# Token inputs laid out by features, the first modulation in two column groups, and a third gate block ahead of the context

## The reference

```python
mx = (silu(c) @ ada_w + ada_b).reshape(6, D)        # modulation of the tokens
mc = (silu(c_ctx) @ ada_w + ada_b).reshape(6, D)    # and of the context
hx = rmsnorm(x,   norm1_g) * (1 + mx[1]) + mx[0]    # x   [512, 1024]
hc = rmsnorm(ctx, norm1_g) * (1 + mc[1]) + mc[0]    # ctx [256, 1024]
ux, uc = hx @ w_in, hc @ w_in                       # gates, values, queries, ...
oc, sc_f, sc_b = hgrn_bidir(*hgrn_inputs(uc, lb), s_zero, s_zero)
ox, _, _       = hgrn_bidir(*hgrn_inputs(ux, lb), sc_f, sc_b)
x = x + mx[2] * merge_branches(ux, hgrn_readout(ux, ox, ...), ...)
x = x + mx[5] * conv_ffn(modulate(rmsnorm(x, norm2_g), mx[3], mx[4]), ...)
x = rmsnorm(x, final_g)
```

## Time and profile before

| | |
|---|---|
| median of three timed runs | 2410.75 us (2410.43 to 2411.60) |
| profiled execution | 2411.24 us |
| its span | 2409.5 us |
| PE busy | 2305.6 us, 96% |
| PEld (weight loads) busy | 1862.6 us, 77% |
| DVE busy | 1395.6 us, 58% |
| ACT busy | 874.8 us, 36% |
| POOL busy | 162.6 us, 7% |
| HBM read | 270.57 MB, 113 GB/s over the span |
| mean granted TensorE clock | 0.984 |

### The profile page before, as it was taken

One profiled execution on the slowest core, in us unless ns is written; L12 is line 12 of the kernel. 1 busy time (PEld: TensorE's weight loads), 2 busy tenths in 40 slices (PEclk: granted clock), 3 DMA queues, 4 the chain that ended last, 5 costly groups with the idle time before them and its releaser, 6 DMA issues.

```text
span 2409.5 us, 29333 instructions
## 1 busy us (share of the span) xinstructions
PE 2305.6 (96%) x10276; PEld 1862.6 (77%) x10276; DVE 1395.6 (58%) x2056; ACT 874.8 (36%) x1168; POOL 162.6 (7%) x96
## 2 busy tenths in 40 slices
PE   7999999989999989999999998999998998999998
PEld 3788888768887868787778776888886886888886
DVE  4556856669999766654745547555435445333322
ACT  4533433245554333323323234443223233443322
POOL 0000000026664000000000000000000000000000
PEclk9999999999999999999999998999999999999999
DMA  6442214413334624142332323666532332333322
GB/s 270 131 136 74 71 57 151 152 57 105 89 102 140 192 80 146 55 129 88 104 116 74 106 79 124 192 190 199 157 93 65 105 96 63 105 94 104 96 88 70
DMA packets 72944, 273.82 MB, mean 114 GB/s; under 512 B 8096, under 2 KB 8480, under 8 KB 71456
## 3 DMA queue, kind: packets, MB, share of 16 engines
q1 hardware_dynamic: 53424, 199.74, 26.7%
q10 hardware_dynamic: 19440, 72.96, 9.6%
HBM read 270.57 MB, written 2.10 MB: 113 GB/s over the span
## 4 chain that ended last, share of the span: by engine, by line
PE 90%; DVE 5%; issue 2%; ACT 2%; DMA 1%; ACTq 0%; DVEq 0%; POOL 0%; SPq 0%
PE bank L424 85%; PE bank L765 1%; PE bank L862 1%; DVE rstd L472 1%; DVE rv_lo L1979 0%; DVE hx_lo L480 0%; PE bank L455 0%; DMA ident<-in_ident 0%; DVE tnorm L487 0%; PE bank L659 0%; PE bank L457 0%; DVE rstd L1799 0%; DVE std L449 0%; DVE rt L1930 0%; PE bank L944 0%
## 5 line engine op out<-in xcount | busy, mean ns | idle before, releaser
L424 PE MATMUL bank<-hx_hi,w_hi 128*128 128x512 f32 x1792 | 711.6, 397 | 40.2 <-DVE hx_lo L480 35.0
L424 PE MATMUL bank<-hx_hi,w_lo 128*128 128x512 f32 x1792 | 704.0, 393 | 0.0
L424 PE MATMUL bank<-hx_lo,w_hi 128*128 128x512 f32 x1792 | 703.9, 393 | 0.0
L383 DVE TENSOR_TENSOR w_lo<-w_raw,w_hi 128x1024 fp32r<-128x1024 f32 x306 | 374.8, 1225 | 495.2 <-ACT w_hi L375 488.9
L375 ACT ACTIVATE w_hi<-w_raw 128x1024 fp32r<-128x1024 f32 x350 | 369.0, 1055 | 458.1 <-PE bank L424 416.3
L424 PEld LDWEIGHTS bank<-hx_hi,w_hi 128*128 128x128 f32 x1792 | 340.7, 190 | 116.6 <-issue 41.1
L424 PEld LDWEIGHTS bank<-hx_hi,w_lo 128*128 128x128 f32 x1792 | 339.9, 190 | 72.4
L424 PEld LDWEIGHTS bank<-hx_lo,w_hi 128*128 128x128 f32 x1792 | 340.6, 190 | 71.0 <-issue 1.2
L1859 DVE SCALAR_TENSOR_TENSOR bank<-zpad,cols,bank 128x512 f32<-128x512 f32 x352 | 233.8, 751 | 11.7 <-ACT bank L1388 11.7
L424 PE MATMUL bank<-hid_hi,w_hi 128*128 128x512 f32 x528 | 210.1, 398 | 1.5 <-POOL hid_lo L2156 1.5
L424 PE MATMUL bank<-hid_lo,w_hi 128*128 128x512 f32 x528 | 209.8, 397 | 0.0
(11 more groups left out here) (305 smaller groups left out, 2752.3 us busy)
## 6 DMA issues: line engine op xcount, KB each, us to landing
w_raw<-in_wstream SPq DMA_DIRECT2D x350, 512.0 KB, 3.6
ada_raw<-in_ada_nk ACTq DMA_DIRECT2D x128, 512.0 KB, 3.7
ada_w<-in_ada_kn SPq DMA_DIRECT2D x8, 1024.0 KB, 18.8
dec<-in_dec ACTq DMA_DIRECT2D x4, 960.0 KB, 4.6
x_tok<-in_x SPq DMA_DIRECT2D x1, 2048.0 KB, 7.8
out_x<-out_tok SPq DMA_DIRECT2D x4, 512.0 KB, 4.0
crow<-in_crow SPq DMA_DIRECT2D x3, 512.0 KB, 23.1
ctx_tok<-in_ctx SPq DMA_DIRECT2D x1, 1024.0 KB, 9.9
```

The source lines that it names most:

```text
L383: nc.vector.tensor_tensor(w_lo[nb.at % RING][:], w_raw[nb.at % RAW][:], w_hi[nb.at % RING][:].bitcast(F32), ALU.subtract).then_inc(lo_read ...
L424: ins = nc.tensor.matmul(out_ap, s, m, start=first and at == 0, stop=last and at == n - 1)
```

## The change

- x, ctx and ctx_2 are stored on the host with features first, in the layout of res, ctx_t and ctx2_t, and loaded there. All transposes of tokens and the copies behind them go (`turn_pe`, jobs 0 to 3 of `context_pe`), and so do the counts "turn" and "turn2".
- The first modulation weights are stored as two column groups (half 0: features 0 to 511 of shift and scale; half 1: the rest) and come in 11 pieces. PE does half 0 for all k, then half 1; before k = 3 of half 1 it sums the squares of x and turns the rows of half 0 (`ada0_turn(0)`). The rows of half 1 are turned inside the first pair, before its k = 2.
- DVE makes modulation and x tiles 0 to 3 for half 0, then 4 to 7 for half 1. ACT has the x tiles in two groups and the context squares between the tiles of the second.
- POOL makes w_lo of the first two blocks and the sums of the context squares. ACT splits weight blocks 0, 1 and 2 at places between the other steps.
- Gate block 2 for x goes into bank bw[0] (third_gate) between the first pair and the context of blocks 0, 1, 2. The context's norm is summed after the pair.
- Of crow, row C is loaded first and gets its Silu before the context tiles; the other two get it in the q stage.
- SP's loads are in a new order; blocks 2 and 3 of the weights are issued outside the loop.
- ctx_2 is loaded after the first column tile of the down projection.

```diff
+ADA0_PARTS = [(0, 0, 1), (0, 1, 1), (0, 2, 1), (0, 3, 1), (0, 4, 2), (0, 6, 2),
+              (1, 0, 2), (1, 2, 1), (1, 3, 1), (1, 4, 2), (1, 6, 2)]
...
-        ada_w0 = sb("ada_w0", [P, KT, 2 * D], F32, r_arena)
+        ada_w0 = sb("ada_w0", [P, 2, KT, 2, L], F32, r_arena)
...
             sp.dma_start(cols[:], cols_in).then_inc(cols_landed, 16)
-            sp.dma_start(x_tok[:], x_in).then_inc(x_landed, 16)
+            for part in ADA0_PARTS[:4]:
+                ada0_load(*part)
             sp.dma_start(ident[:], ident_in).then_inc(ident_landed, 16)
-            sp.dma_start(ctx_tok[:], ctx1_in).then_inc(ctx_landed, 16)
-            for k in range(KT):
-                sp.dma_start(ada_w0[:, k, :], ada_kn[k]).then_inc(ada0_in[k], 16)
-                if k == KT // 2:
-                    for s in range(RAW):
-                        sp.dma_start(w_raw[s][:], wstream[s]).then_inc(raw_ready[s], 16)
-            for n in range(3):
-                sp.dma_start(crow[:, n, :], crow_in[n:n + 1, :].to_broadcast([P, D])).then_inc(crow_landed, 16)
+            w_load(0)
+            for part in ADA0_PARTS[4:7]:
+                ada0_load(*part)
+            x_load(0)
+            ada0_load(*ADA0_PARTS[7])
+            x_load(1)
+            x_load(2)
+            ada0_load(*ADA0_PARTS[8])
+            w_load(1)
+            for part in ADA0_PARTS[9:]:
+                ada0_load(*part)
+            sp.dma_start(ctx_t[:], ctx1_in).then_inc(ctx_landed, 16)
+            w_load(2)
+            crow_load(ROW_C, crow_c_landed)
+            w_load(3)
             sp.dma_start(dft1[:], dft1_in).then_inc(dft1_landed, 16)
             sp.dma_start(masks[:], masks_in).then_inc(masks_landed, 16)
+            for row in (ROW_C2, ROW_CTX2):
+                crow_load(row, crow_landed)
...
+            pe.wait_ge(scol_ready, 1)
+            for k in range(KT):
+                ada0_pe(0, k)
+            for k in range(KT):
+                if k == 3:
                     pe.wait_ge(consts, 2)
                     norm_pe(pe, n1x, L, bn)
-                    norm_pe(pe, n1c, LC, bank[4])
...
+                    pe.wait_ge(ident_landed, 16)
+                    ada0_turn(0)
+                ada0_pe(1, k)
...
+            pair_pe(pe, n1x, pair, False, lambda k: ada0_turn(1) if k == 2 else None)
+            norm_pe(pe, n1c, LC, bank[4])
+            pe.wait_ge(ada0_ready, 1)
+            gate_x(2, third_gate)
+            for n in range(3):
+                gate_ctx(n, Block(B_GATES + n))
+            for n in range(3, 8):
+                gate_x(n, take_x(pe, JX["gates"] + n))
+                b = Block(B_GATES + n)
                 gate_ctx(n, b)
...
+            split_hi(act, Block(1 - AHEAD))
+            norm_root(act, n1x, L, bn)
...
+            x_hi(range(4))
+            act.wait_ge(ada0_mm, 3)
+            nc.scalar.activation(ada_rows[:, 2 * L:3 * L], ada_banks[2][:2, :], ACT.Copy).then_inc(ada0_rows, 1)
+            split_hi(act, Block(2 - AHEAD))
+            act.wait_ge(ctx_landed, 16)
+            for j in range(3):
+                square(act, n1c, j, ctx_t, LC)
+            for j in range(4, KT):
+                x_hi((j,))
+                square(act, n1c, j - 1, ctx_t, LC)
+            square(act, n1c, KT - 1, ctx_t, LC)
+            norm_root(act, n1c, LC, bank[4])
+            ada_load(act, 0)
+            act.wait_ge(crow_c_landed, 16)
+            nc.scalar.activation(crow[:, ROW_C, :], crow[:, ROW_C, :], ACT.Silu).then_inc(crow_silu, 1)
             norm_hi(act, n1c, LC, lambda j: ada0[:, j, 1:2], hc_hi)
...
+            for half in range(2):
+                if half == 1:
+                    dve.wait_ge(ada0_mm, 4)
+                    nc.vector.tensor_copy(ada_rows[:, 3 * L:], ada_banks[3][:2, :]).then_inc(ada0_rows, 1)
+                modulation0(half)
+                norm_lo(dve, n1x, res, L, lambda j: mod_a[:, 0, j:j + 1], lambda j: ada0[:, j, 0:1], hx_hi, hx_lo,
+                        range(4 * half, 4 * half + 4))
+            dve.wait_ge(lo_ready, RAW)
             for b in range(RAW, AHEAD):
                 split_lo(dve, Block(b - AHEAD))
+            norm_rec(dve, n1c, LC)
+            norm_lo(dve, n1c, ctx_t, LC, lambda j: mod_a[:, 1, j:j + 1], lambda j: ada0[:, j, 1:2], hc_hi, hc_lo)
...
+            for b in range(RAW):
+                pool.wait_ge(hi_ready, b + 1)
+                nc.gpsimd.tensor_tensor(w_lo[b][:], w_raw[b][:], w_hi[b][:].bitcast(F32), ALU.subtract).then_inc(lo_ready, 1)
+            for j in range(1, KT - 1):
+                pool.wait_ge(n1c.sq_ready, j + 1)
+                if j >= 2:
+                    pool.wait_ge(n1c.summed, j - 1)
+                nc.gpsimd.tensor_tensor(n1c.std[:, :LC], n1c.std[:, :LC], n1c.sq[j % 2][:, :LC], ALU.add)\
+                    .then_inc(n1c.summed, 1)
...
+                if job == 0:
+                    act.wait_ge(hid_l, 2 + HT)
+                    act.dma_start(ctx2_t[:], ctx2_in).then_inc(ctx2_landed, 16)
                 if job == 4:
+                    act.wait_ge(ctx2_landed, 16)
...
-        "ada_kn": ada_w[0][:, :2 * D].reshape(KT, P, 2 * D),
+        "ada_kn": ada_w[0][:, :2 * D].reshape(KT, P, 2, 2, L).transpose(3, 1, 0, 2, 4),
...
-        "x": inputs["x"][0].reshape(LT, P, D).transpose(1, 0, 2),
+        "x": inputs["x"][0].T.reshape(KT, P, L).transpose(1, 0, 2),
```

More of the change, by code:

```diff
@@ L482, in rest @@
                                                op1=ALU.subtract).then_inc(nm.lo, 1)
-            for j in range(KT):
+            for j in js:
                 if j >= 2:
@@ L651, in _ @@
             sp.wait_ge(out_stored, 16 * LT)
-        def turn_pe(pe, src_tok, dst_tiles, take, job0, done):
-            for j in range(KT):
-                b = take(pe, job0 + j)
-                for t in range(dst_tiles):
-                    ins = nc.tensor.transpose(b[:, t * P:(t + 1) * P], src_tok[:, t, j * P:(j + 1) * P], ident[:])
-                ins.then_inc(done, 1)
         def none(j):
@@ L684, in program, with pair_pe @@
         down_done = {B_DOWN: sem("down_done0"), B_SD0: sem("down_done1"), B_SD1: sem("down_done2")}
-        def pair_pe(pe, nm, pair, ends=True):
+        def pair_pe(pe, nm, pair, ends=True, beside=none):
             for b, _ in pair:
@@ L1207, in _, with x_hi @@
-            norm_hi(act, n1x, L, lambda j: ada0[:, j, 0:1], hx_hi)
-            norm_hi(act, n1c, LC, lambda j: ada0[:, j, 1:2], hc_hi)
-            for b in range(RAW, AHEAD):
-                split_hi(act, Block(b - AHEAD))
-            ada_load(act, 0)
-            act.wait_ge(crow_landed, 48)
-            nc.scalar.activation(crow[:], crow[:], ACT.Silu).then_inc(crow_silu, 1)
+            split_hi(act, Block(1 - AHEAD))
+            norm_root(act, n1x, L, bn)
+            def x_hi(js):
+                norm_hi(act, n1x, L, lambda j: ada0[:, j, 0:1], hx_hi, js)
@@ L1249, in _ @@
                 ins.then_inc(x_free, 1)
+                if n == 0:
+                    act.wait_ge(crow_landed, 32)
+                if n < 2:
+                    row = (ROW_C2, ROW_CTX2)[n]
+                    nc.scalar.activation(crow[:, row, :], crow[:, row, :], ACT.Silu).then_inc(crow_silu, 1)
             for g in range(4):
```

170 lines of the change are left out of this document (72 added, 98 removed).

## The result

The changed kernel takes 2382.57 us (median of four runs, 2380.47 to 2385.59) against 2410.59 for the kernel before on the same chip: ratio 0.9889, 95% interval 0.9873 to 0.9904. The forecast was 2384, range 2379 to 2392. The profiled execution took 2380.47 us, with a span of 2378.7.

What follows compares the result with a forecast made beforehand. It took TensorE (PE), carrying 90% of the chain of waits, as the bound: 2411.24 - 22.3 (head) - 6.3 (second context) + 1.9 (collisions) = 2384.5 us, 2384 against the median; range 2379 to 2392.

Steps and rivals of the forecast that it cites:

- the head: Start of the kernel, 0 to 90 us: gate block 3 starts at 67.7 instead of 90.03, gain 22.3 us before collisions.
- the second context: Down projection: without its load wait and transposes, 5.2 us saved at the start and 1.05 at later transposes, together 6.3.
- byte n lands at 3.05 + n/0.42: Loads in the head: n in MB, time in us, at a steady 0.42 MB/us; x lands from 19.7 to 24.0.
- rival D: Rival, chance 0.02: smaller load pieces stream slowly in the head; at 150 GB/s 46 us more, total 2430.
- both waits end before DVE would be ready anyway: First pair of gate blocks: PE's wait for the second transposes and ACT's for its row copy cost nothing.
- The collision: Head: POOL's six additions of context squares slow DVE's x tiles, between 0 and 3.8 us, taken as 1.9 lost.
- SP's stops: Load queue in the head: SP waits for a w_lo before weight blocks 2 and 3, costed at nothing.
- the two rows of Silu in the q stage: Moved from the head: some 1.2 us each on ACT beside 5.5 us of PE, costed at nothing; uncovered 2.4.
- A: Rival, chance 0.20: clock falls behind the context tiles, contexts 1 and 2 at half rate, 2.9 us more, total 2386.5.
- B: Rival, chance 0.12 with E: the down projection keeps its loss through low clock or late weights, up to 6.3, 2390.
- C: Rival, chance 0.05: all 64 first-modulation records in the head run at half rate, 28 us more, 2412, no change.
- E: Rival, chance 0.12 with B: the head's third gate block covers nothing, its w_lo being late; at worst 5.5 us, 2389.5.

Runs made afterwards that it cites:

- pool_small: Changed kernel with GpSimd's six additions of context squares cut to 8 of 256 columns (output wrong): ratio to before 0.9882, gate block 3 at 68.90 us.
- ctx2_later: Kernel before with the second context still transposed, but one column tile later in the down projection: ratio to before 0.9962.
- no_third: Changed kernel with gate block 2 for x moved behind the context of blocks 0 and 1: ratio to before 0.9898, gate block 3 at 77.83 us.
- ctx2_only: Kernel before with only the second context changed: loaded by features after the down projection's first column tile, not transposed. Ratio to before 0.9977.
- after_again: The changed kernel unaltered, measured again beside the kernel before on one chip: median 2385.70 us against 2411.02, ratio 0.9900.
- early_ctx: Changed kernel with the context loaded, squared and normed earlier, and the second block's w_lo moved from GpSimd to VectorE: median 2382.70 us, ratio to before 0.9875.
- x_first: Changed kernel with x loaded ahead of all pieces of the modulation: ratio to before 0.9908, gate block 3 at 75.19 us.
- big_first: Changed kernel with the first eight row blocks of modulation half 0 loaded in three pieces instead of six: ratio to before 0.9890, gate block 3 at 71.39 us.
- layout_order: Kernel before with x and first context loaded by features, and four modulation rows loaded ahead of them: ratio to before 0.9968, gate block 3 at 82.28 us.

## Why the prediction was right, step by step

The total was right, and so was the mechanism of its large terms. Against the profiled execution: forecast 2384.5, measured 2380.47. The difference has three parts: the head gave 1.35 us less, the second context 0.24 more, and 5.2 came where I had put nothing. The change's own part was forecast at 26.7 and measured at 25.6.

*The head.* Forecast with collisions 22.3 - 1.9 = 20.4 us, measured 19.08.

| step | forecast, us | measured |
|---|---|---|
| first modulation matmul | 5.2 | 5.93 |
| x landed, squares begin | 19.7 | 21.13 |
| first x tile | 34.0 | 34.77 |
| modulation done | 38.1 | 39.4 |
| second rows turned | 41.65 | 42.95 |
| pair done, with 1.9 of collisions | 51.9 | 53.42 |
| gate block 3, with 1.9 | 69.6 | 70.95 |

The 1.35 us at the end arose in two steps. First, x landed 1.4 us later: the step "byte n lands at 3.05 + n/0.42" took before's early rate, and the new queue moved 344 GB/s from 3 to 9 us and not 416. This is rival D in a mild form, against which I had cited slices of 34 to 40 us, which say nothing about the first ones. (344 for 416 over 6 us is 0.43 MB, 1.0 us at the later rate; the other 0.4 is not taken apart.) (DMA in 0 to 45 us, to be held against the earlier trace rows.)

```profile
GB/s 0 102 306 376 339 295 353 352 394 437 437 437 408 437 415 426 410 401 421 419 404 408 408 430 433 430 401 437 422 408 397 404 411 401 401 414 404 251 4 0
```

Of it 0.4 us was given back at the root, for which I had reckoned 0.7 us behind the weight split (it starts 0.34 us behind the sum), and 0.25 by small operations that took 0.27 us and not 0.5. Second, "both waits end before DVE would be ready anyway" was wrong for the second transposes: they stand behind the six matmuls of k = 1, start at 42.30 and not at 41.70, and DVE is idle for 1.29 us. This is 0.6 us more than I had. The rest ran as laid out, to a tenth or two: reciprocal, four tiles, context tiles, PE following DVE in gaps of 0.3 us. Only the end of the pair didn't: it came 1.98 us behind the last hx_lo and not 1.5; tenths saved before and after it made that good.

*The collision.* Taken at 1.9 between 0 and 3.8, measured 1.9 by pool_small. That my halving met it is luck; the trace shows why it is about half. A DVE operation is stretched only when it meets a POOL operation, and some of the six additions fell into DVE's waits. Where they met, the three tile operations lost 0.35, 0.47 and 0.49 us, most of the 0.56 to 0.69 us that the addition then running still had to go. The POOL operations took 0.72 us where DVE was idle, and not 0.63: I had halved the duration of twice as many columns, but part of it doesn't go with the columns; with 8 of them, in pool_small, they still took 0.20. The longer ones, up to 1.06 here and 0.53 there, met DVE operations and were held up by them.

*The second context.* Forecast 6.3, measured 6.54 and, alone, 6.54. The 13th matmul as the end of the low clock was the right one to count from. The first group of transposes was inside it, and ctx2_later gives all four groups 1.74, 0.43 each, against my 0.35.

*Edits costed at nothing.* For SP's stops, the two rows of Silu in the q stage, and the load of the second context beside the stream, the markers behind show nothing lost (410.51 against 410.86, and 111.07 in a stage without the wait).

*The rivals.* A (clock falls behind the context tiles): it did not, 1.00 through 56 to 68. But no_third shows that the danger was near: with 4.09 us of idle before the tiles, the same pattern ran at 0.50. My 2.9 us for it was wrong by its own working: 2.9 us is one context at full clock, so two at half rate would take 5.8 more; the stretch at 0.50 in no_third cost 1.9. B: the down stage has 1.00 behind the 1.47 us gap. C (modulation at low clock): only the first records.

```profile
L781 PE MATMUL bank<-ada_w,scol x64: 592/592/1057, 5.9 to 38.8; 128*2 128x512 f32 x64
```

In the three traces with the transposes ahead of them (before, ctx2_only, ctx2_later) all 64 took 589 to 593 ns; in the ten without, the first four to seven were slow, the slowest 1057 to 1062. So the transposes had paid for PE's way up to its full speed, and I was right to charge 2 us for it: the first 44 records took 20.60 us, at before's pace 19.1, so 1.5 lost. The Trainium skill, "TensorE: Matmul & The Clock Gate", Part 4, says that transposes don't count as PE activity in the way that matmuls do. The trace of before, whose transposes are float32, disagrees: they took PE from 477 to 272 ns and left the modulation at full speed. E: the third block's w_lo was ready at 53.1 and PE wanted it at 54.1, so it covered; the reserve was one microsecond.

*The rest.* I expected both kernels alike behind the head and the down stage. The profiled executions differ there by 5.2 us, and the medians of the first comparison (28.0 us) hold some of it; after_again's 25.3 does not. That the forecast of 26.7 lies between is partly luck. The 0.2% (4.8 us) that I called the limit of a measurement is of the size of this spread.

## What to carry over

Where PE's own work fills a stage, lay the loads in the order in which PE can use them, and put the work that frees another engine's chain first; then see which piece of PE work can stand in front of each chain: here a block of 5.5 us was worth 6, since it covered a gap and kept the clock. Judge such edits by a marker in the trace right behind the stage, not by the total, when the total moves by 5 us with the clock. And when DVE's chain of operations with two inputs is critical, keep POOL's additions from beside it: place them beside a reciprocal.

## What the hardware showed beyond that

- *POOL and DVE.* tnorm, hx_lo, mod_a and w_lo, all with two or more inputs in SBUF, are held up by POOL's additions (0.75 to 1.10 and 1.24, 0.17 to 0.67, 1.23 to 1.65 us). The reciprocal isn't: 3.35 us beside three additions of 0.72 us each in early_ctx (31.82 to 35.17), as in the earlier trace rows with none; the x tiles behind it there, under the last additions, took up to 1.21 and not 0.75. The Trainium skill, "SBUF — State Buffer", "Who interferes with whom", says that a DVE instruction with at most one SBUF input, outside the two-port modes, doesn't contend with GpSimd. For the reciprocal, which reads one tile, the trace agrees.
- *The clock column at the start.* It reads 1.00 from the first microsecond in every trace, while the modulation's first records take 924 to 1057 ns against 592. It isn't a measurement there: the changed kernel's trace has its first record of the granted clock at 9.1 us (1.00, during the last of the slow matmuls), before's at 12.9 (among the transposes), and the column gives 1.00 where there is none. The low level of the first microseconds shows only in the durations.

```profile
L781 PE MATMUL bank<-ada_w,scol x4: 924/1034/1057, 5.9 to 8.4; 128*2 128x512 f32 x4
```

```profile
7.00:8.00 1.00, 1.00 (x2) 0.13 (x1) 0.00 (x0) 0.00 (x0) 0.00 (x0) 1.00 0.96 336
```

- *DMA's first microseconds.* With all engines busy (0.99 to 1.03), 3 to 9 us moved 344 GB/s with first pieces of 4 KB per partition (changed kernel), 343 with 6 KB (x_first), 378 with 4, then 12 and 16 KB (big_first), and 416 with 16 KB (before); from 9 to 20 us it was 421, 417 and 424 in the changed kernel, big_first and before. Executions differ: the changed kernel's order of loads gave 318 to 350 in five traces (0.92 to 0.99 busy), x first in 16 KB 396 to 416 in four. layout_order, which begins with rows of 8 KB, moved 413. Why small pieces are slower only at the start is open.
- *The clock behind a stall.* Behind the same wait of 3.06 us the sum ran at 0.50 in eight traces and at 1.00 in five. What decides it isn't in these traces.
